# Three groups of the sparse branch's gate, run between the first conditioning products

## The reference, cut to what matters

```
ada = silu(c) @ w_ada + b_ada              # 6 x 2048 columns: shift, scale, gate, twice
h   = RMSNorm(x) * (1 + scale1) + shift1
(qkv, z, a, b, dq, dk, dv, iq, ik, iw, gate_gdn, gate_dsa) = split(h @ w_in)
o_gdn = gated DeltaNet(qkv, a, b, z)       # chunked delta rule
o_dsa = top-k sparse attention(dq, dk, dv, iq, ik, iw)
mix = sigmoid(gate_gdn) * (o_gdn @ w_gdn_out) + sigmoid(gate_dsa) * (o_dsa @ w_dsa_out)
x  += gate1 * (mix @ w_o)                  # then the ConvFFN in the same manner, final RMSNorm
```

## Time and profile before

| | |
|---|---|
| Median of three runs | 1941.8 us |
| The profiled execution | 1940.12 us, of it a span of 1938.3 us from the first to the last instruction |
| TensorE busy | 97% of the span, mean granted clock 0.981 |
| ScalarE, VectorE, GpSimd busy | 41%, 33%, 61% |
| HBM read | 379.70 MB |
| First matmul, end of the last conditioning slot, first slot with h | 5.05, 94.06 and 95.89 us |

### The profile page before, as it was taken

How to read it: one execution, slowest core, us unless ns; L and a number is a source line. 1 busy time by engine, 2 the same in 40 slices (tenths; PEclk the granted TensorE clock), 3 DMA queues, 4 the chain that set the end, 5 groups by cost and what they waited for, 6 DMA issues and landing times.

```text
span 1938.3 us, 41659 instructions
## 1 busy us (share of the span) xinstructions
PE 1878.8 (97%) x16742; PEld 1754.7 (91%) x16742; DVE 634.9 (33%) x1782; ACT 802.0 (41%) x1345; POOL 1185.4 (61%) x508
## 2 busy tenths in 40 slices
PE   6799999999999999999999899999999999999997
PEld 2299999999888878887999899999999999999996
DVE  1355635444232332423343422321123321123333
ACT  1454356654223232323434555543344443344442
POOL 0076656664444344434877577777777777777773
PEclk7799999999999999999999999999999999999998
DMA  9966444454787878787855354454444545544552
GB/s 392 409 236 215 145 135 146 148 174 156 269 290 262 292 244 291 237 291 261 231 190 169 124 169 167 162 165 169 165 163 166 168 163 164 167 168 162 164 186 85
DMA packets 145102, 390.69 MB, mean 202 GB/s; under 512 B 27522, under 2 KB 36162, under 8 KB 144322
## 3 DMA queue, kind: packets, MB, share of 16 engines
q1 hardware_dynamic: 124976, 374.01, 56.8%
q10 hardware_dynamic: 19986, 14.70, 2.5%
HBM read 379.70 MB, written 8.88 MB: 200 GB/s over the span
## 4 chain that ended last, share of the span: by engine, by line
PE 90%; DMA 5%; DVE 2%; ACT 1%; issue 1%; POOL 0%; DVEq 0%; ACTq 0%; SPq 0%; POOLq 0%; PEldq 0%
PE bank L2254 27%; PE bank L2255 26%; PE bank L2259 26%; PE bank L2229 3%; DMA raw_a<-in_stream 3%; DMA raw_c<-in_stream 1%; PE bank L2738 1%; PE bank L2205 1%; PE bank L2218 1%; DMA raw_b<-in_stream 0%; DMA raw_m<-in_stream 0%; PE bank L2623 0%; PE bank L2322 0%; PE bank L2607 0%; PE bank L2467 0%
## 5 line engine op out<-in xcount | busy, mean ns | idle before, releaser
L749 POOL TENSOR_TENSOR rest_a<-raw_a,hi_a 128x1024 fp32r<-128x1024 f32 x174 | 417.1, 2400 | 339.8 <-ACT hi_a L807 339.8
L2254 PE MATMUL bank<-h_hi,hi_a 128*128 128x288 f32 x1752 | 481.7, 301 | 1.9 <-ACT hi_a L807 1.8
L2255 PE MATMUL bank<-h_lo,hi_a 128*128 128x288 f32 x1752 | 471.0, 295 | 0.0
L2254 PEld LDWEIGHTS bank<-h_hi,hi_a 128*128 128x128 f32 x1752 | 328.9, 188 | 19.8 <-issue 15.8
L2255 PEld LDWEIGHTS bank<-h_lo,hi_a 128*128 128x128 f32 x1752 | 329.6, 188 | 0.4
L807 ACT ACTIVATE hi_a<-raw_a 128x1024 fp32r<-128x1024 f32 x174 | 184.2, 1059 | 296.3 <-PE bank L2259 221.5
L749 POOL TENSOR_TENSOR rest_b<-raw_b,hi_a 128x1024 fp32r<-128x1024 f32 x78 | 187.3, 2402 | 122.4 <-ACT hi_a L807 122.4
L2259 PE MATMUL bank<-h_hi,rest_a 128*128 128x288 f32 x1544 | 236.0, 295 | 2.8 <-POOL rest_a L749 2.8
L2259 PEld LDWEIGHTS bank<-h_hi,rest_a 128*128 128x128 f32 x1544 | 215.8, 189 | 3.3 <-POOL rest_a L749 3.3
L2254 PE MATMUL bank<-h_hi,hi_b 128*128 128x288 f32 x616 | 167.8, 299 | 0.0
L749 POOL TENSOR_TENSOR rest_a<-raw_a,hi_b 128x1024 fp32r<-128x1024 f32 x56 | 134.0, 2393 | 52.9 <-ACT hi_b L807 52.9
(11 more groups left out here) (511 smaller groups left out, 3695.7 us busy)
## 6 DMA issues: line engine op xcount, KB each, us to landing
raw_a<-in_stream SPq DMA_DIRECT2D x376, 512.0 KB, 3.5
raw_b<-in_stream SPq DMA_DIRECT2D x185, 512.0 KB, 3.5
raw_c<-in_stream SPq DMA_DIRECT2D x94, 512.0 KB, 3.3
raw_m<-in_stream SPq DMA_DIRECT2D x29, 512.0 KB, 6.0
st<-in_state ACTq DMA_DIRECT2D x8, 512.0 KB, 6.0
st<-in_state SPq DMA_DIRECT2D x8, 512.0 KB, 5.9
out_state_s<-st ACTq DMA_DIRECT2D x8, 512.0 KB, 7.2
x<-in_x SPq DMA_DIRECT2D x2, 1152.0 KB, 13.7
```

The lines of the kernel that those rows point to most:

```text
L749: nc.gpsimd.tensor_tensor(rest_in(name, r), raw_of(name, r), w_hi[q].bitcast(f32), ALU.subtract).then_inc(lo_ready, 1)
L2254: MM(banks[c][:, 0:N], w_, hi_of(k), start=(first and k == 0), stop=False)
L2255: ins = MM(banks[c][:, 0:N], w_, lo_of(k), start=False, stop=False)
```

## The change

Twelve D-slots, the four quarters of the first three gate_dsa groups, become "early" slots and leave the mix stage, where 68 D-slots remain in a new order ("ds" of groups 0, 1 and 2 come first) and the filling pattern has one D less in three repeats of four. Early slot e is group e % 3, quarter e // 3. Slots 0 to 5 run ahead of conditioning groups 7 to 12, slot 6 ahead of group 14, slots 7 to 11 behind the last conditioning slot, with `turn(15)` between 7 and 8. The first nine are loaded in the first stage, each three places ahead of its turn; the last three at the head of the next stretch of the ring. x is loaded behind slots 2 and 4, its squares are summed in groups 2 and 3, and h is made from group 5 on. The conditioning products move from banks 0 to 3 to banks 4 and 5, with the bias added after each group and not after each two; the three early groups stand in banks 0 to 3, 6 and 7. ScalarE copies the finished sums from PSUM to `park`, which the first two groups of the input projection and `weights_t` wait for, and takes their sigmoids three groups before the end of that stage (`early_gates`). The squares for the L2 norms of q and k get two buffers in other places.

```diff
+N_EARLY = 3
+EARLY = [(e % N_EARLY, e // N_EARLY) for e in range(N_EARLY * (KT // KS))]
+EARLY_AT = {(7, 0): (0,), (8, 0): (1,), (9, 0): (2,), (10, 0): (3,), (11, 0): (4,), (12, 0): (5,), (14, 0): (6,), (15, 4): (7, 8)}
+E_IN = N_EARLY * (KT // KS - 1)
+LEAD = 3
+
+
+def first_loads():
+
+    run = []
+    for n in range(2 * KT // CT):
+        for s_ in range(KT // KS + 1):
+            run += [("early", e) for e in EARLY_AT.get((n, s_), ())]
+            if s_ < KT // KS:
+                run.append(("ada1", 4 * n + s_))
+    for e in range(E_IN):
+        p = run.index(("early", e))
+        run.insert(max(0, p - LEAD), run.pop(p))
+    return run
+
+
+FIRST = first_loads()
+FIRST_AT = {what: p for p, what in enumerate(FIRST)}
...
-NA, ND = 4 * KT // CT * (KT // KS), (KT // CT) * (2 * (KT // KS) + H // KS)
-FILL = "DAADAADAADAAD" * (ND // 5)
-D_GROUPS = [g for m in range(KT // CT) for g in (("gd", m, KT // KS), ("ds", m, H // KS))] + [("gg", m, KT // KS) for m in range(KT // CT)]
+NA, ND = 4 * KT // CT * (KT // KS), (KT // CT) * (2 * (KT // KS) + H // KS) - len(EARLY)
+FILL = ("DAADAADAADAA" * 3 + "DAADAADAADAAD") * (ND // 17)
+D_GROUPS = [g for m in range(KT // CT) for g in (("gd", m, KT // KS), ("ds", m, H // KS)) if m >= N_EARLY or g[0] == "ds"] \
+    + [("gg", m, KT // KS) for m in range(KT // CT)]
...
+BASE["in"] = len(FIRST)
+BASE["mix"] = BASE["in"] + len(EARLY) - E_IN + 4 * N_IN
...
-        for first, end, size in ((0, BASE["in"], RAW), (BASE["in"], BASE["ada2"], RAW_I), (BASE["mix"], BASE["go"], RAW_M), (BASE["go"], NSLOTS, RAW)):
+        for first, end, size in ((0, BASE["in"], RAW), (BASE["in"], BASE["mix"], RAW_I), (BASE["mix"], BASE["go"], RAW_M), (BASE["go"], NSLOTS, RAW)):
...
-                    for j in range(BASE["in"]):
-                        r, use = raw_at("ada1", j)
-                        load_one(r, use, ada_slot(j))
-                        if j in (9, 13):
-                            k0, done = (0, x_in) if j == 9 else (KT // 2, x_in2)
+                    for what in FIRST:
+                        r, use = raw_at(*what)
+                        load_one(r, use, ada_slot(what[1]) if what[0] == "ada1" else early_slot(what[1]))
+                        if what in (("ada1", 2), ("ada1", 4)):
+                            k0, done = (0, x_in) if what[1] == 2 else (KT // 2, x_in2)
                             sp.dma_start(x[:, k0:k0 + KT // 2, :].rearrange("p k n -> p (k n)"),
                                          A["x"][:, k0 * N:(k0 + KT // 2) * N]).then_inc(done, 16)
                     continue
                 if n == 1:
+                    for e in range(E_IN, len(EARLY)):
+                        r, use = raw_at("early", e)
+                        load_one(r, use, early_slot(e))
...
+            def keep_early(g):
+
+                r, use = raw_at("early", len(EARLY) - N_EARLY + g)
+                act.wait_ge(raw_free[r], use + 2)
+                for c in range(CT):
+                    last = A_(park[CT * g + c], bank[E_BANK[g] + c][:, 0:N], ACT.Copy)
+                last.then_inc(parked, 1)
+
+            def early_gates():
+
+                act.wait_ge(X["o"], UNITS)
+                for g in range(N_EARLY):
+                    for c in range(CT):
+                        last = A_(pd[:, CT * g + c, :], park[CT * g + c], ACT.Sigmoid)
+                    last.then_inc(g_sig, 1)
+
+            for q in range(4):
+                square_quad(q)
+            act.wait_ge(const_in, 48)
+            rms(0)
+            round_pair(0)
+            round_pair(1)
+            round_samples(0)
+            hi("early", 0)
+            round_pair(2)
+            hi("early", 1)
+            hi("early", 2)
+            round_pair(3)
+            round_samples(1)
+            hi("early", 3)
+            round_pair(4)
+            hi("early", 4)
+            hi("early", 5)
+            round_pair(5)
+            round_samples(2)
+            hi("early", 6)
+            round_pair(6)
+            for e in (7, 8, 9):
+                hi("early", e)
+            round_pair(7)
             round_samples(3)
+            hi("early", 10)
+            hi("early", 11)
+            for g in range(N_EARLY):
+                hi("in", g)
+                keep_early(g)
...
+                if n == N_IN - 4:
+                    early_gates()
...
+                CP(cond_2[n % 2][:, :], bank[4 + n % 2][:, 0:CT * P]).then_inc(cond_cp, 1)
+
+            def cond_bias(n):
+
+                m, q = divmod(n, 2)
+                k = 2 * m + q * KT
+                dve.wait_ge(cond_done, n + 1)
+                T_(ada[:, k:k + CT, :], bank[4 + q][:, CT * P:CT * P + CT * NCP].rearrange("p (c n) -> p c n", c=CT)[:, :, 0:NC],
+                   vec[:, V_BADA + k:V_BADA + k + CT].unsqueeze(2).to_broadcast([P, CT, NC]), ALU.add).then_inc(bias_done, 1)
+                if q:
+                    dve.drain()
+                    STT(amul[:, k - KT:k - KT + CT, :], ada[:, k:k + CT, :], 1.0,
+                        vec[:, V_G1 + k - KT:V_G1 + k - KT + CT].unsqueeze(2).to_broadcast([P, CT, NC]), ALU.add, ALU.mult).then_inc(h_t, 1)
...
+            def early(e):
+
+                g, s_ = EARLY[e]
+                if (g, s_) == (2, 0):
+                    pe.wait_ge(xr_ready, 4)
+                pe.wait_ge(hs_lo, s_ + 1)
+                pe.wait_ge(h_hi_ready, (s_ + 1) * KS)
+                slot("early", e, lambda k: h_hi[:, s_ * KS + k, :], lambda k: h_lo[:, s_ * KS + k, :], (bank[E_BANK[g]], bank[E_BANK[g] + 1]),
+                     s_ == 0, s_ == KT // KS - 1, tiles=HB + s_ * KS)
+
...
+                    for e in EARLY_AT.get((n, s_), ()):
+                        early(e)
...
+            early(E_IN - 2)
+            turn(2 * KT // CT - 1)
+            for e in range(E_IN - 1, len(EARLY)):
+                early(e)
...
+                pe.wait_ge(parked, N_EARLY)
...
-                    if n == 0:
-                        pe.wait_ge(hs_lo, s_ + 1)
-                        pe.wait_ge(h_lo_ready, HB + (s_ + 1) * KS)
-                        pe.wait_ge(h_hi_ready, (s_ + 1) * KS)
-                    if (n, s_) == (0, 0):
-                        pe.wait_ge(cond_cp, 2 * KT // CT + 1)
-                    if (n, s_) == (0, 1):
-                        turn(2 * KT // CT - 1)
+                    if s_ == 0 and n < 2:
+                        pe.wait_ge(parked, n + 1)
```

More of the change, by code:

```diff
@@ L70 @@
 NSLOTS = _b
-BASE["in"] = BASE["small"]
 N_DSA, N_Z, N_QKV, N_IN = 1, 1 + DSA_T // CT, (DSA_T + Z_T) // CT, 1 + (DSA_T + Z_T + QKV_T) // CT
@@ L424, in decoder_step @@
         assert gp.at <= rest_at
[L425 to L426 removed]
+        sq_ = Place(rest_at + 4 * CT * N_EARLY * N)
+        sqp_k = sq_.take("sqp_k", [P, H, SEQ])
         sqs = sq_.take("sqs", [P, 2 * H, NS])
@@ L432, in decoder_step @@
         kmask = gq.take("kmask", [P, DB, P])
+        sqp_2 = (sqp_k, Place(gq.at).take("sqp_q", [P, H, SEQ]))
         qkd = gq.take("qkd", [P, 4, P])
@@ L435, in decoder_step @@
         u_t = gq.take("u_t", [P, 2, P])
+        assert gq.at >= tp.at
+        park_a = Place(gq.at).take("park_a", [P, CT * N_EARLY - 1, N])
+        park = [park_a[:, t, :] for t in range(CT * N_EARLY - 1)] + [qkv[:, QKV_T - 4, :]]
+        assert gq.at + 4 * (CT * N_EARLY - 1) * N <= nc.sbuf_usable_end
         st_p = gq.take("st_p", [P, 2, P])
@@ L567, in raw_at @@
         def raw_at(name, j, i=0, per=0):
-            s_ = BASE[name] + j
+            s_ = BASE[name] + j if name not in ("ada1", "early", "in") else BASE["in"] + len(EARLY) - E_IN + j if name == "in" \
+                else FIRST_AT[name, j] if (name, j) in FIRST_AT else BASE["in"] + j - E_IN
             first, _, size, before = next(t for t in stretches if t[0] <= s_ < t[1])
@@ L754, in run @@
                         lo(name, first + j, i, per)
+            for e in range(len(EARLY)):
+                lo("early", e)
             for j in range(4 * N_IN):
@@ L1368, in _ @@
                     cond_copy(n - 1)
-                if n >= 3 and n % 2 == 1:
-                    if n == 3:
+                    if n == 1:
                         dve.wait_ge(const_in, 48)
-                    cond_bias((n - 3) // 2)
-                if n > PAIR_AT:
-                    lo_pair(n - PAIR_AT - 1)
-                if n - 2 in SAMPLE_AT:
-                    lo_samples(SAMPLE_AT[n - 2])
-                if SQUARE_AT <= n < SQUARE_AT + 4:
-                    add_squares(n - SQUARE_AT)
-                if XR_AT <= n < XR_AT + 4:
-                    if n == XR_AT:
-                        dve.wait_ge(rs_ready, 1)
-                    scale_x(n - XR_AT)
-                if n in SAMPLE_AT:
-                    samples(SAMPLE_AT[n])
+                    cond_bias(n - 1)
+                if n in (2, 3):
+                    add_squares(2 * n - 4)
+                    add_squares(2 * n - 3)
+                if n in (4, 5):
+                    if n == 4:
+                        dve.wait_ge(rs_ready, 1)
```

(16 more changed lines are left out.)

75 lines of the change are left out of this document (26 added, 49 removed).

## The result

| | before | after |
|---|---|---|
| Median | 1941.01 us (1939.03 to 1945.79, 4 runs) | 1958.55 us (1956.04 to 1962.52, 4 runs) |
| The profiled execution: span | 1938.3 us | 1955.7 us |
| Mean granted clock | 0.981 | 0.982 |

The ratio is 1.0089, with an interval of [1.0074, 1.0103]. The change makes the kernel slower by 17.5 us, where no change was forecast, and the time lies above the range of 1930 to 1957. The prediction was wrong.

A forecast was written before the change was run, and what follows sets the result against it. TensorE was taken to bound the kernel, loads its first stage; 22.1 us there plus 15.1 for the slots behind, less 37.4 from the mix stage, gave -0.2 us, no change: 1942 us, range 1930 to 1957.

The forecast's parts named there:

- What bounds the kernel: Whole kernel: TensorE, busy 97% of the span, except the first stage, bound by loads until 94.06 us.
- what leaves the mix stage: Mix stage: twelve D-slots of 3.37 us, 40.4 us, less 3 us for lost cover; gain 37.4 us.
- the 3 us that I took off for lost cover: Mix stage: waits the moved D-slots had covered, put between 0 and 17 us and taken as 3.
- rival 4: Mix stage: it needs the cover, 17 us and not 3, so slower at 1956 us; chance 0.12.
- The mix stage 37 us shorter: Mix stage: a sign named in advance, its length in the trace falling by 37 us.
- What the ring costs: First stage: seven inner early slots hold buffers, each costing 0.95 us of DMA time, 6.7 in all; bounds 0 and 14 us.
- Slot 4: First stage: early slot 4 comes 0.9 us late, its `hi` standing behind `round_pair(4)` on ScalarE.
- The clock: First stage: one of seven inner early slots at the half level, 3 us; bounds 0 and 23 us.
- Rival 3: First stage: half clock under the early slots, 3.3 us each, slower, 1962 us with all seven; chance 0.18.
- The second bound: First stage: all seven inner early slots at the half clock level, 7 x 3.3 = 23 us.
- The five slots behind: Behind the last conditioning slot: early slots 7 to 11 take 17.7 us, less 2.6, so 15.1 us more.
- Costed at nothing: Several stages: x at slots 2 and 4, sixteen bias additions, copies to `park`, sigmoids and table loads, all at 0 us.

The follow-up runs named there:

- e2_ring: Changed kernel with the last three early slots counted into the first stage's ring, so the input projection's stretch has 100 slots, not 103; 1946.15 us.
- e3_tail: As e2_ring, but all twelve early slots run behind the last conditioning slot and none inside; 1937.31 us.
- e5_best: Changed kernel with early loads one place ahead instead of three, a 100-slot stretch, and ScalarE splitting slots 3 and 4 before rounding pair 4; 1931.66 us.
- e6_warm: Changed kernel plus two extra unread matmuls behind each of the first three conditioning products of groups from 5 on; 1954.79 us.
- e4_noearly: Changed kernel without early slots, all 80 D-slots in the mix stage in the old order, the rest of the change kept; 1941.85 us.
- e11_warm_gaps: e10_behind plus two extra unread matmuls behind each of the first three conditioning products of groups 5, 6, 13, 14 and 15; 1928.71 us.
- e10_behind: e5_best with early slot 8's load moved behind the last conditioning load instead of ahead of it; 1931.20 us.
- e8_lead5: Changed kernel with each early slot's load five places ahead of its use instead of three; 1989.63 us.

## Why the prediction was wrong, by its own steps

**What bounds the kernel, what leaves the mix stage: right.** With the ring's stretch at 100 slots the mix stage is 41.3 us shorter (e2_ring), 42.0 (e3_tail) and 41.5 (e5_best), against 40.4 for the twelve slots alone. So the 3 us that I took off for lost cover were nothing, and rival 4 (17 us) is out.

**The step that is missing: 10.8 us.** The mix stage gave 30.4 and not 37.4. I had divided the place of one early slot by the ring's size to find its buffer (number 0, place 72) but did not do it at the other end of the stretch, where three more slots put the last one into the buffer that the next stage loads first. With the wrong count of groups (87 slots, the last use of buffer 0 at place 84) I would not have seen it, but I had not looked at all. "The mix stage 37 us shorter" was the sentence that the trace refuted.

**"What the ring costs", the step that failed: 0.95 us was 2.3.** The mechanism was right: the eighth load goes out when the early slot ends. Its terms were too small. I took 3.3 us for the slot, 3.3 for a landing and 0.62 for the product, 7.3 us with the 0.1 for the issue. The first five cycles were (92.72 - 49.27) / 5 = 8.69 us in the mean: 4.0 for the slot, 3.9 from its end to the product behind the landing, 0.8 from there to the next slot. The slots took 3.45 to 4.74, because they often begin at the half level. The landings took 3.5 to 4.7, 3.8 in the mean; my 3.3 came from a quiet stage. With 4.0 and 3.8 my own formula gives 4.45 + 4.0 + 0.1 + 3.8 - 10.2 = 2.15, and against the 6.4 of loads it was 2.3 for each cycle, 11.6 in all. The sixth (92.72 to 106.77) and the seventh (106.77 to 122.74) are 2.6 and 3.2 us longer than their nine and ten loads. So the seven slots cost 17.4 us beside their loads, and with 11.5 for the nine loads that is the 29 us measured. I had 10.6 for them (6.7, 3 for the clock, 0.9 for slot 4). I also took the bubble as a given, and did not ask what it would be for another lead. The lead of three is its cause: with one place the first three periods are 0.1 us over the loads in the mean, and with five places the first five are 7.4 over them.

**Slot 4: right in mechanism, and 0.5 us instead of 0.9.** The ring's loop takes longer than its 8.2 us, so most of the chain on ScalarE is hidden, but not all of it. In the changed kernel:

```profile
83.70 0.62 PE L2302 MATMUL bank<-raw_a,c_f 128*10 128x256 f32 x8 [1.68 <-DMA raw_a<-in_stream]
84.83 0.37 PE L2335 MATMUL bank<-h_hi,hi_a 128*128 128x288 f32 x1 [0.51 <-ACT hi_a L850]
```

The product is over at 84.32, and slot 4 waits 0.51 us more for `hi`. These 0.5 us are part of its period of 9.22 and of the 17.4 above. At one place of lead it stands alone, 8.34, and changing the order on ScalarE removes it.

**The clock: the value was about right, and by luck.** The seven inner slots took 3.3 us more than in e6_warm, and I had 3. But I had one slot at the half level throughout; in the trace four began at it and went over (3.90, 4.74, 4.33 and 4.12 us), and with the full clock the last product came only 1.4 us earlier. Rival 3 gave 1962, near the measured 1958.6, but not for its reason: it wants seven slots of 6.6 us, and the longest in the changed kernel took 4.74. The rule that I had weighed there (the Trainium skill, TensorE: Matmul & The Clock Gate, HAM oscillation) agrees with the trace in that the clock falls again and again between loads. The second bound that I drew from it does not: a slot of 24 matmuls that began at the half level went over to the full one inside itself. Of the 2.3 us of a cycle some 1.8 are left at the full clock (8.22 against 6.4), but this is an estimate, since the extra matmuls of e6_warm take time of their own and the waits for the landing were 0.3 us longer there.

**The five slots behind: 2.4 us short.** Slot 7 began at the half level and took 4.57 us with `turn(15)`, not 3.7: 0.9 of the 2.4. From slot 8 to 9 it was 5.78 us, not 4.5: 1.3. I gave `amul` the 0.32 us of the earlier trace rows and took 2.38 for the next instruction, `hs`, from the same rows. Both are short instructions (0.18 and 0.29 us in e5_best); in the kernel before it was `hs` that met a GpSimd split and waited it out. Here it was `amul`, on the chain to slot 9. The 3.4 us from the end of `amul` to that of `lo_samples` were misread too: the earlier trace rows has 3.6 (100.60 to 104.24).

**Costed at nothing: right as far as it can be told.** e4_noearly shows it for all but the sigmoids and the copies to `park`. The input projection's stage is 1.0 us longer in the changed kernel, and equally so in e4_noearly (351.5 us), which has neither; e3_tail and e5_best have both and took 350.4, and e2_ring took 353.5. So 1 us is within what this stage differs from trace to trace.

**Numbers.** Forecast -0.2 us, measured +17.3: first stage 7.0, the slots behind it 2.4, the input projection 1.0, mix stage 7.0, rest 0.2. The chance of 0.29 for slower stood mostly on seven slots at the half clock and on lost cover, and neither came; the range's upper end of 1957 was too low by one term that I did not have, and my upper bound for the ring (14 us, seven times 2.05) was passed by the 17.4 measured, the clock included.

## What to carry to other kernels

When a slot that is held long is put into a ring of loads, write down which load goes out only when it is released, and which piece of work needs that load. If the next long slot stands behind it, as with three places of lead here, the loop of slot, landing and product sets the pace (8.69 us a cycle against 6.4 of loads), though bandwidth is free. If it does not, count whether the loads still on their way last as long as the slot and the next landing. Loading later, just early enough for the split, can be faster than loading earlier. Whenever slots are added to a stretch of a ring that is counted anew at its end, take the last places modulo the ring's size and see which buffer the next stage asks for first.

## What the runs showed of the hardware

- A VectorE instruction on 128 x 18 elements took 0.18 us with GpSimd idle and 2.17 us beside a GpSimd subtraction of 2.40 us that had begun 0.26 us earlier, and both ended within 0.03 us. The Trainium skill (SBUF — State Buffer, SBUF: two separate sides) says that VectorE with two SBUF inputs and GpSimd hold a shared pair of ports one at a time, for a whole instruction. The trace agrees. In the kernel before it is `hs` that took 2.38 us, beside a split that had begun 0.17 us earlier (100.52), and 0.29 in e5_best.
- In this load-bound stage a slot of 24 matmuls that began at 1.2 GHz went over to 2.4 GHz inside itself (3.7 to 5.8 us instead of 3.45; matmuls 0.24 and then 0.13 us apart). With extra matmuls in the waits the granted clock of 44 to 107 us was 1.00 instead of 0.90 (e11_warm_gaps, e10_behind).
- A load of 512 KB issued when an early slot ended, with others right behind it, landed 3.2 us after its issue (97.85 in e8_lead5, with nothing else on its way) or 4.7 (69.92 in the changed kernel, where loads issued before were still on their way), against a median of 9.1 in the full queue of before. In that queue the DMA engines moved 407 to 411 GB/s in each window of 4 us from 40 to 96 us.
